# The last stage of a decoder step moved into the experts' phase, with four of nine tiles summed by TensorE products

## The chip, the cores and the metric

The kernel runs on one core of a Trainium2 chip. The metric is the device time of one execution in microseconds (us). The kernel before was timed in three runs; one more execution was profiled.

## The reference, cut to what matters

One step of a hybrid decoder layer over 1024 prompt rows and 64 sample rows, all of width 1024. After the token mixers and the memory attention comes a mixture of experts, and then a last norm:

```
eid, comb = hier_route(hn, ...)          # two experts of 32 for each row, and their two weights
h = h + routed_experts(hn, eid, comb, w_e_gate, w_e_up, w_e_down)
y = rmsnorm(h, g_final)                  # h * rsqrt(mean(h*h) + EPS) * g_final
```

For each row the last stage computes h + c0 * y1 + c1 * y2, where y1 and y2 are the results of the row's two experts, and then scales the row by its root mean square and by g_final. Everything before this stage is the same in both kernels.

## The kernel before, in words

The 1088 rows lie in TILES = 9 tiles of P = 128 rows; the last holds 64 rows. `build` calls phases one after the other; between two stands `core.end_phase()` (L129), which clears the semaphores and lets all engines meet at a barrier. Each phase's block ends with a meeting of the engines too.

`phase_experts` (L2324) runs the 32 experts. Each gets one block of 128 gathered rows; its result `y` is copied by ScalarE (L2626) and stored to `blocks` in HBM by ScalarE's DMA queue (L2628), with a count on `y_stored0` or `y_stored1`. Rows beyond 128 of one expert would go to extra blocks: `over_blocks` (L2355) is a loop of NOVER = 16 rounds on each engine, with a branch around its body in each round, taken where there is no such block. Here there is none, so each engine goes through 16 rounds that do nothing. TensorE goes through them after its last product (L2537), VectorE after L2590, ScalarE after its last store (L2677), GpSimd much earlier (L2446). SyncE loads h into `h_rows` (L2411) and g_final into `g_rows` (L2412) at the end of the phase. ScalarE waits for the last stores at L2679.

`phase_combine` (L2682) is the last stage. GpSimd issues 18 indirect DMAs (L2704), two for each tile, which gather y1 and y2 from `blocks` into SBUF, and only then, behind them in its own queue, the nine small powers (L2710, mean square to the power -0.5). VectorE's order is written out: for tile t `add(t)` (L2719 and L2720, each one operation over 1024 columns), `mean_square(t - 1)` (L2724), `gain(t - 2)` (L2729). ScalarE squares and sums a tile (L2751) and scales it (L2746, `normed`). SyncE stores each tile when `gain` is done (L2697).

Before the change VectorE's part of one tile is:

```
lk(v.scalar_tensor_tensor(h[r, t], y1[r, t], comb[r, 0, t:t + 1], h[r, t], ALU.mult, ALU.add))
v.scalar_tensor_tensor(h[r, t], y2[r, t], comb[r, 1, t:t + 1], h[r, t], ALU.mult, ALU.add)
v.tensor_tensor(o[r, t], o[r, t], gf[r], ALU.mult)
```

Of the kernel before, what the change touches and what calls it, by code (L numbers as in the profile page):

```python
# [13 lines left out]
ALU = mybir.AluOpType  # L14
ACT = mybir.ActivationFunctionType
AX = mybir.AxisListType
F32 = mybir.dt.float32
# [3 lines left out]
P = 128  # L21
D = 1024
KC = D // P
SEQ = 1024
DB, DS = 8, 8
NS = DB * DS
# [2294 lines left out]
                ins.then_inc(S_("table"), 1)  # L2321


def phase_experts(core, PS, slot_tok, over_info, raw, wg_hi, wg_lo, h_rows, g_rows):  # L2324

# [9 lines left out]
    GU, DN = range(0, 4), range(4, 6)  # L2335
    with ExitStack() as ctx:
        sb = lambda n, s, t=F32: ctx.enter_context(nc.sbuf_tensor("ex_" + n, s, t))
        wd_hi, wd_lo = sb("wd_hi", [P, len(DN), PW], F32R), sb("wd_lo", [P, len(DN), PW], F32R)
        w_hi = lambda j: wg_hi[:, j] if j in GU else wd_hi[:, j - len(GU)]
        w_lo = lambda j: wg_lo[:, j] if j in GU else wd_lo[:, j - len(GU)]  # L2340
        xg = sb("xg", [P, 2, D])
        x_hi, x_lo = sb("x_hi", [P, 2, KC, P], F32R), sb("x_lo", [P, 2, KC, P], F32R)
# [44 lines left out]
        with nc.Block() as block:  # L2387
            @block.sync
            def _(sp):
                sp.dma_start(ident[:], d["ident"]).then_inc(S_("ident"), 16)  # L2390
                for j in range(NP):
                    sp.sem_inc(S_(f"w{j}"), 16)

                def load_gu(n, freed):
                    for j in GU:
                        sp.wait_ge(S_("w_split"), freed(j))
                        sp.dma_start(raw[:, j], expert_piece(d, j, n)).then_inc(S_(f"w{j}"), 16)

                def load_dn(n):
                    for j in DN:  # L2400
                        sp.wait_ge(S_("w_split"), done_dn(n - 1, j))
                        sp.dma_start(raw[:, j], expert_piece(d, j, n)).then_inc(S_(f"w{j}"), 16)

                load_gu(1, lambda j: j + 1)
                with sp.Fori(2, NE) as n:
                    load_gu(n, lambda j: done_gu(n - 1, j))
                    load_dn(n - 1)
                load_dn(NE - 1)
                sp.wait_ge(S_("w_used"), done_gu(LAST, GU[-1]))
                for t in range(TILES):  # L2410
# [10 lines left out]
                sp.wait_ge(S_("h_rows"), 16 * (TILES + 1))  # L2421

            @block.gpsimd
            def _(po):
# [15 lines left out]
                def over(j):  # L2440
                    po.wait_ge(S_("ov_turned"), j)
                    po.tensor_copy(idx[:, 0:1], slot_tok[:, bass.ds(j + NE, 1)]).then_inc(S_("ov_idx"), 1)
                    po.wait_ge(S_("ov_idx"), j + 1)
                    po.sem_inc(S_("passed"), 1)
                    po.indirect_dma_start(xg[:, 0], None, d["hn"], bass.IndirectOffsetOnAxis(ap=idx[:, 0:1], axis=0)).then_inc(S_("ov_rows"), 16)
                over_blocks(po, over)  # L2446

            @block.tensor
            def _(pe):
# [85 lines left out]
                    ins.then_inc(S_("ov_d"), 1)  # L2535
                pe.wait_ge(S_("y"), NE + 1)
                over_blocks(pe, over)  # L2537

            @block.vector
            def _(v):  # L2540
# [51 lines left out]
                def over(j):  # L2592
# [5 lines left out]
                    v.wait_ge(S_("ov_d"), j)  # L2598
                    v.tensor_copy(hT[:], h_in()).then_inc(S_("ov_hT"), 1)
                over_blocks(v, over)  # L2600

            @block.scalar
            def _(act):
# [74 lines left out]
                for par in range(2):  # L2678
                    act.wait_ge(S_(f"y_stored{par}"), 16 * (NE // 2) + 16)  # L2679


def phase_combine(core, PS, dest, comb, h, gf):  # L2682

    nc, d, sem = core.nc, core.dram, core.sem
    S_ = lambda n: sem("cb_" + n)
    with ExitStack() as ctx:
        sb = lambda n, s, t=F32: ctx.enter_context(nc.sbuf_tensor("cb_" + n, s, t))
        y1, y2, o = sb("y1", [P, TILES, D]), sb("y2", [P, TILES, D]), sb("o", [P, TILES, D])
        expo, st = sb("expo", [P, 1]), sb("st", [P, TILES, 4])
        rows = [P if t < NT else NS for t in range(TILES)]  # L2690
        with nc.Block() as block:  # L2691
            @block.sync
            def _(sp):
                for t in range(TILES):
                    sp.wait_ge(S_("out"), t + 1)
                    dst = d["y_p"][t * P:(t + 1) * P, :] if t < NT else d["y_s"]
                    sp.dma_start(dst, o[0:rows[t], t]).then_inc(S_("stored"), 16)  # L2697
                sp.wait_ge(S_("stored"), 16 * TILES)

            @block.gpsimd  # L2700
            def _(po):
                for t in range(TILES):
                    for k, y in enumerate((y1, y2)):
                        po.indirect_dma_start(y[0:rows[t], t], None, d["blocks"],  # L2704
                                              bass.IndirectOffsetOnAxis(ap=dest[0:rows[t], k, t:t + 1], axis=0)).then_inc(S_(f"y{t}"), 16)
                po.memset(expo[:], -0.5).then_inc(S_("expo"), 1)  # L2706
                po.wait_ge(S_("expo"), 1)
                for t in range(TILES):
                    po.wait_ge(S_("ms"), t + 1)
                    po.tensor_tensor(st[:, t, 2:3], st[:, t, 1:2], expo[:], ALU.pow).then_inc(S_("rstd"), 1)  # L2710

            @block.vector
            def _(v):
                lk = Steps(v, S_("dve"))

                def add(t):
                    r = slice(0, rows[t])
                    v.wait_ge(S_(f"y{t}"), 32)
                    lk(v.scalar_tensor_tensor(h[r, t], y1[r, t], comb[r, 0, t:t + 1], h[r, t], ALU.mult, ALU.add))  # L2719
                    v.scalar_tensor_tensor(h[r, t], y2[r, t], comb[r, 1, t:t + 1], h[r, t], ALU.mult, ALU.add).then_inc(S_("added"), 1)  # L2720

                def mean_square(t):
                    v.wait_ge(S_("squares"), t + 1)
                    v.tensor_scalar(st[:, t, 1:2], st[:, t, 0:1], 1.0 / D, EPS, ALU.mult, ALU.add).then_inc(S_("ms"), 1)  # L2724

                def gain(t):
                    r = slice(0, rows[t])
                    v.wait_ge(S_("normed"), t + 1)
                    v.tensor_tensor(o[r, t], o[r, t], gf[r], ALU.mult).then_inc(S_("out"), 1)  # L2729

                for t in range(TILES):
                    add(t)
                    if t >= 1:
                        mean_square(t - 1)
                    if t >= 2:
                        gain(t - 2)
                mean_square(TILES - 1)
                gain(TILES - 2)
                gain(TILES - 1)

            @block.scalar
            def _(act):
                def normed(t):
                    r = slice(0, rows[t])
                    act.wait_ge(S_("rstd"), t + 1)
                    act.activation(o[r, t], h[r, t], ACT.Copy, scale=st[r, t, 2:3]).then_inc(S_("normed"), 1)  # L2746

                for t in range(TILES):
                    act.wait_ge(S_("added"), t + 1)

                    act.activation(y1[:, t], h[:, t], ACT.Square, accum_out=st[:, t, 0:1]).then_inc(S_("squares"), 1)  # L2751
                    if t >= 1:
                        normed(t - 1)
                normed(TILES - 1)


def build(nc, dram):
    with ExitStack() as ctx:
# [16 lines left out]
        dest, comb = sb("dest", [P, 2, TILES], I32), sb("comb", [P, 2, TILES], F32)  # L2775
        slot_tok, over_info = sb("slot_tok", [P, NBLK], I32), sb("over_info", [P, NOVER + 1], I32)
        with ExitStack() as weights:
            wg_hi, wg_lo = [weights.enter_context(nc.sbuf_tensor("ex_" + n, [P, 4, PW], F32R)) for n in ("wg_hi", "wg_lo")]
        h_rows, g_rows, rest = sb("h_rows", [P, TILES, D], F32), sb("g_rows", [P, D], F32), sb("rest", [P, 6, D], F32)
        with ExitStack() as experts:  # L2780
            raw = experts.enter_context(nc.sbuf_tensor("moe_raw", [P, len(PIECES), PW], F32))
            phase_route(core, PS, dest, comb, slot_tok, over_info, raw)
            core.end_phase()
            phase_experts(core, PS, slot_tok, over_info, raw, wg_hi, wg_lo, h_rows, g_rows)
            core.end_phase()
        phase_combine(core, PS, dest, comb, h_rows, g_rows)


SCRATCH = {"proj": ((ROWS, NIN), F32), "mu_shift": ((DB, NRW), F32), "pm": ((ROWS + 8, NRW), F32), "mixed": ((ROWS, D), F32), "h2": ((ROWS, D), F32),
# [57 lines left out]
```

## Time and profile before

| | us |
|---|---|
| median of 3 runs | 2061.6 (2060.19 to 2062.38) |
| profiled execution, its own time | 2058.51 |
| its span in the profile | 2056.7 |
| PE busy | 1797.1 (87%) |
| DVE busy | 1195.4 (58%) |
| ACT busy | 824.9 (40%) |
| POOL busy | 339.8 (17%) |

PE is TensorE, PEld its weight loads, DVE is VectorE, ACT ScalarE, POOL GpSimd and SP SyncE; a "q" behind a name is that engine's sequencer, which handles branches, waits and the issue of DMAs. Times inside the span are us from its start; lengths in "min/median/max" are ns. The granted clock (PEclk) is a share of TensorE's full 2.4 GHz: 1.00 is that, 0.50 is 1.2 GHz.

### The profile page before, as it was taken

The page shows a single profiled execution, that of the slowest core. Times are in us where ns is not written, and L with a number is a line of the kernel's source. Part 1 is how long each engine was busy: PE and PEld are TensorE (multiplying, and loading weights), DVE is VectorE, ACT ScalarE, POOL GpSimd, SP SyncE. Part 2 cuts the span into 40 slices and gives each one's busy share as a digit, 9 for nine tenths or more (in the row PEclk, how much of TensorE's full clock was granted, in tenths as well). Part 3 has the DMA queues.
Part 4 walks back from the last instruction along what each step waited for, and adds up shares of the span by engine and source line. Part 5 has one row for each costly group of instructions (what it writes and reads, how often), then busy time and mean ns, then how long its engine had stood idle before and what let it go on. Part 6 is the DMA issues. An engine that isn't in the chain of part 4 may idle for free. (4 is left out here: it accounts for less than half of the span.)

```text
span 2056.7 us, 35509 instructions
## 1 busy us (share of the span) xinstructions
PE 1797.1 (87%) x14826; PEld 1477.8 (72%) x14826; DVE 1195.4 (58%) x1320; ACT 824.9 (40%) x930; POOL 339.8 (17%) x307
## 2 busy tenths in 40 slices
PE   7999997988888976899999998728999999999940
PEld 7998885777777755787888885327888888888830
DVE  4533103677777655424333331168989999999926
ACT  5111212434333314302212120017777777777713
POOL 1322002343333420000000000011111111111004
PEclk9999998999999977999999999859999999999975
DMA  7765253222223128552011126159999999999856
GB/s 286 236 201 178 95 166 88 66 72 72 93 76 96 54 57 292 207 196 101 31 42 53 37 102 254 59 206 348 404 405 400 404 401 401 405 401 405 327 190 244
DMA packets 111973, 419.12 MB, mean 204 GB/s; under 512 B 25892, under 2 KB 44264, under 8 KB 82920
## 3 DMA queue, kind: packets, MB, share of 16 engines
q1 hardware_dynamic: 99592, 373.76, 48.7%
q0 software_dynamic: 7072, 25.69, 3.3%
q10 hardware_dynamic: 5184, 17.82, 2.1%
q8 instruction: 100, 1.64, 0.3%
q14 instruction: 25, 0.20, 0.0%
HBM read 350.10 MB, written 75.53 MB: 207 GB/s over the span
## 5 line engine op out<-in xcount | busy, mean ns | idle before, releaser
L2544 DVE TENSOR_TENSOR ex_wg_lo<-moe_raw,ex_wg_hi 128x2048 fp32r<-128x2048 f32 x128 | 287.4, 2284 | 10.7 <-ACT ex_wg_hi L2609 10.5
L2609 ACT CAST ex_wg_hi<-moe_raw 128x2048 fp32r<-128x2048 f32 x128 | 244.6, 1913 | 80.3 <-PE banks L2454 55.4
L2454 PE MATMUL banks<-ex_wg_hi,ex_x_hi 128*128 128x512 f32 x512 | 207.8, 406 | 11.2 <-issue 6.9
L2454 PE MATMUL banks<-ex_wg_hi,ex_x_lo 128*128 128x512 f32 x512 | 201.9, 394 | 0.0
L2454 PE MATMUL banks<-ex_wg_lo,ex_x_hi 128*128 128x512 f32 x512 | 201.2, 393 | 0.0
L2544 DVE TENSOR_TENSOR ex_wd_lo<-moe_raw,ex_wd_hi 128x2048 fp32r<-128x2048 f32 x64 | 146.3, 2288 | 56.0 <-ACT ex_wd_hi L2609 56.0
L2609 ACT CAST ex_wd_hi<-moe_raw 128x2048 fp32r<-128x2048 f32 x64 | 122.3, 1912 | 52.8 <-PE banks L2454 34.1
L2454 PEld LDWEIGHTS banks<-ex_wg_hi,ex_x_hi 128*128 128x128 f32 x512 | 97.3, 190 | 43.1 <-issue 22.1
L516 PE MATMUL banks<-pj_w_hi,pj_x_hi 128*128 128x448 f32 (+1 forms) x288 | 109.7, 381 | 11.2 <-DVE pj_x_lo L347 11.2
L2454 PEld LDWEIGHTS banks<-ex_wg_hi,ex_x_lo 128*128 128x128 f32 x512 | 97.1, 190 | 21.2
L2454 PEld LDWEIGHTS banks<-ex_wg_lo,ex_x_hi 128*128 128x128 f32 x512 | 97.5, 191 | 18.5
L516 PE MATMUL banks<-pj_w_lo,pj_x_hi 128*128 128x448 f32 (+1 forms) x288 | 109.4, 380 | 0.0
L2454 PE MATMUL banks<-ex_wd_hi,ex_h_hi 128*128 128x512 f32 x256 | 102.4, 400 | 6.0 <-DVE ex_h_lo L2556 6.0
L2454 PE MATMUL banks<-ex_wd_hi,ex_h_lo 128*128 128x512 f32 x256 | 102.3, 400 | 0.0
L2454 PE MATMUL banks<-ex_wd_lo,ex_h_hi 128*128 128x512 f32 x256 | 102.1, 399 | 0.0
L2426 POOL COPY ex_idx<-moe_slot_tok 128x1 int32 (+1 forms) x32 | 25.3, 791 | 461.5 <-PE banks L2364 415.5
L1595 POOL TENSOR_TENSOR at_st<-at_st,at_expo 128x1 f32<-128x1 f32 x18 | 9.7, 542 | 532.8 <-DVE at_st L1631 532.8
L516 PE MATMUL banks<-pj_w_hi,pj_x_lo 128*128 128x448 f32 (+1 forms) x256 | 97.4, 380 | 0.0
L1108 PE MATMUL banks<-mx_TTT,mx_X 64*64 64x64 f32 x1344 | 77.6, 224 | 4.6 <-DVE mx_X L744 1.5
L516 PE MATMUL banks<-pj_odd_lo,pj_x_hi 128*128 128x448 f32 (+1 forms) x216 | 81.6, 378 | 0.0
L516 PE MATMUL banks<-pj_odd_hi,pj_x_hi 128*128 128x448 f32 (+1 forms) x216 | 81.6, 378 | 0.0
L1017 ACT COPY mx_TTT<-banks 128x512 f32<-128x512 f32 (+1 forms) x84 | 45.3, 540 | 89.9 <-PE banks L1108 89.0
(403 smaller groups left out, 4111.6 us busy)
## 6 DMA issues: line engine op xcount, KB each, us to landing
moe_raw<-w_e_gate SPq DMA_DIRECT2D x64, 1024.0 KB, 7.8
moe_raw<-w_e_up SPq DMA_DIRECT2D x64, 1024.0 KB, 7.3
moe_raw<-w_e_down SPq DMA_DIRECT2D x64, 1024.0 KB, 7.7
blocks<-ex_y ACTq DMA_DIRECT2D x32, 512.0 KB, 7.8
mx_pin<-proj SPq DMA_DIRECT2D x8, 1664.0 KB, 6.9
h<-at_h SPq DMA_DIRECT2D x18, 512.0 KB, 2.7
at_slots<-cache_mem_k SPq DMA_DIRECT2D x8, 1024.0 KB, 12.0
at_slots<-cache_mem_v SPq DMA_DIRECT2D x8, 1024.0 KB, 7.4
```

The costliest lines, as they stand in the source:

```text
L516: ins = pe.matmul(PS[:, n % 8, 0:width], xs[:, t, k, :], ws[c % 2][:, k, 0:width], start=k == 0 and a == 0, stop=k == KC - 1 and a == len( ...
L1017: act.copy(TTT[:, g].rearrange("p x m t -> p (x m t)")[:, 0:n], PS[:, 2 + g, 0:n]).then_inc(S_("T_ready"), 1)
L1108: return pe.matmul(out, a, b, start=start, stop=stop, skip_group_check=True)
L1595: po.tensor_tensor(rstd_c(par), ms_c(par), expo[:, 0:1], ALU.pow).then_inc(S_(kind + "_rstd"), 1)
L2426: po.tensor_copy(idx[:, bf:bf + 1], slot_tok[:, bass.ds(n, 1)]).then_inc(S_("idx"), 1)
L2454: ins = pe.matmul(out, a, b, start=first and i == 0, stop=final and i == 2)
L2544: v.tensor_tensor(w_lo(j), raw[:, j], as_f32(w_hi(j)), ALU.subtract).then_inc(S_("w_split"), 1)
L2609: act.copy(w_hi(j), raw[:, j]).then_inc(S_("w_high"), 1)
```

## The change

`phase_combine` is gone, and so is the `end_phase` before it; its work stands at the end of `phase_experts`. GpSimd waits for the stores of `blocks` itself, then issues the same 18 gathers and the nine powers. VectorE makes eight diagonal matrices (a row weight times the identity) while it has nothing else, adds five tiles (0, 1, 3, 5, 8) as before, and finishes all tiles with one operation, `scaled(t)`, that multiplies by the row's factor and by g_final together; it comes BEHIND = 5 tiles after the add. ScalarE only squares. For tiles 2, 4, 6 and 7 TensorE forms the sum in PSUM with six f32 products of 512 columns: identity by h, diagonal by y1, diagonal by y2, for each half of the columns. `h_rows`, `g_rows`, `y1` and `y2` lie where the split weights lay.

```
+            @block.gpsimd                       (behind over_blocks)
+                for par in range(2):
+                    po.wait_ge(S_(f"y_stored{par}"), 16 * (NE // 2) + 16)
+                for t in range(TILES):
+                    for k, y in enumerate((y1, y2)):
+                        po.indirect_dma_start(y[0:rows[t], t], None, d["blocks"],
+                                              bass.IndirectOffsetOnAxis(ap=dest[0:rows[t], k, t:t + 1], axis=0)).then_inc(S_(f"y{t}"), 16)
+                po.memset(expo[:], -0.5).then_inc(S_("expo"), 1)
+                po.wait_ge(S_("expo"), 1)
+                for t in range(TILES):
+                    po.wait_ge(S_("ms"), t + 1)
+                    po.tensor_tensor(st[:, t, 2:3], st[:, t, 1:2], expo[:], ALU.pow).then_inc(S_("rstd"), 1)
...
+            @block.tensor                       (behind over_blocks)
+                pe.wait_ge(S_("h_rows"), 16 * (TILES + 1))
+                pe.wait_ge(S_("dg"), 2 * len(ON_PE))
+                for n, t in enumerate(ON_PE):
+                    pe.wait_ge(S_(f"y{t}"), 32)
+                    for hf in range(2):
+                        cols = slice(hf * 512, hf * 512 + 512)
+                        pe.matmul(pair_of(t)[:, hf, :], ident[:], h_rows[:, t, cols], start=True, stop=False)
+                        pe.matmul(pair_of(t)[:, hf, :], dg[:, n, 0, :], y1[:, t, cols], start=False, stop=False)
+                        ins = pe.matmul(pair_of(t)[:, hf, :], dg[:, n, 1, :], y2[:, t, cols], start=False, stop=True)
+                    ins.then_inc(S_("summed"), 1)
...
+            @block.vector                       (behind over_blocks)
+                def scaled(t):
+                    r = slice(0, rows[t])
+                    v.wait_ge(S_("rstd"), t + 1)
+                    src = pair_of(t).rearrange("p a n -> p (a n)") if t in ON_PE else h_rows[r, t]
+                    v.scalar_tensor_tensor(h_rows[r, t], src, st[r, t, 2:3], g_rows[r], ALU.mult, ALU.mult).then_inc(S_("out"), 1)
+                for n, t in enumerate(ON_PE):
+                    for k in range(2):
+                        v.tensor_scalar(dg[:, n, k, :], ident[:], comb[:, k, t:t + 1], None, ALU.mult).then_inc(S_("dg"), 1)
+                v.wait_ge(S_("h_rows"), 16 * (TILES + 1))
+                for t in range(TILES):
+                    if t not in ON_PE:
+                        add(t)
+                    if t >= 1:
+                        mean_square(t - 1)
+                    if t >= BEHIND:
+                        scaled(t - BEHIND)
+                mean_square(TILES - 1)
+                for t in range(TILES - BEHIND, TILES):
+                    scaled(t)
...
+            @block.scalar                       (behind over_blocks; the waits for y_stored are gone here)
+                for t in range(TILES):
+                    if t in ON_PE:
+                        act.wait_ge(S_("summed"), ON_PE.index(t) + 1)
+                    else:
+                        act.wait_ge(S_("added"), t + 1 - sum(u < t for u in ON_PE))
+                    act.activation(y1[:, t], pair_of(t).rearrange("p a n -> p (a n)") if t in ON_PE else h_rows[:, t], ACT.Square, accum_out=st[:, t, 0:1]).then_inc(S_("squares"), 1)
...
-            phase_experts(core, PS, slot_tok, over_info, raw, wg_hi, wg_lo, h_rows, g_rows)
-            core.end_phase()
-        phase_combine(core, PS, dest, comb, h_rows, g_rows)
+            phase_experts(core, PS, slot_tok, over_info, dest, comb, raw, split, final)
```

`add` and `mean_square` are the functions of before. How the rows of the program move is seen at three places. On GpSimd, at the end of the experts' phase; over_info is the number of extra blocks. Before:

```order
L2358 REGISTER_ALU
L2358 COMPARE_AND_BRANCH
L2387 UNCONDITIONAL_BRANCH
L131 ISA [waits barrier_Pool_Activation_PE_DVE_SP_gather]
L2700 UNCONDITIONAL_BRANCH [waits barrier_Pool_Activation_PE_DVE_SP_gather]
L2704 DMA cb_y1<-blocks,moe_dest 128x1024
L2704 DMA cb_y2<-blocks,moe_dest 128x1024
```

Now (the semaphores in brackets bear names of an earlier phase, whose numbers they took over; they are the two `y_stored`):

```order
L2364 REGISTER_ALU
L2364 COMPARE_AND_BRANCH
L2462 DMA moe_y1<-blocks,moe_dest 128x1024 [waits pj_stored4,pj_stored3]
L2462 DMA moe_y2<-blocks,moe_dest 128x1024
```

The first gather no longer stands behind a barrier of all five engines, only behind the two store counts.

On VectorE, in the middle of the last stage. Before, one round of the steady order:

```order
L2719 SCALAR_TENSOR_TENSOR moe_h_rows<-cb_y,moe_comb,moe_h_rows 128x1024
L2720 SCALAR_TENSOR_TENSOR moe_h_rows<-cb_y,moe_comb,moe_h_rows 128x1024
L2724 TENSOR_SCALAR cb_st<-cb_st 128x1
L2729 TENSOR_TENSOR cb_o<-cb_o,moe_g_rows 128x1024
```

Now, from the add of tile 5 to the end (L2650 is `scaled`; its input `banks` is PSUM):

```order
L2639 SCALAR_TENSOR_TENSOR moe_h_rows<-moe_y,moe_comb,moe_h_rows 128x1024
L2640 SCALAR_TENSOR_TENSOR moe_h_rows<-moe_y,moe_comb,moe_h_rows 128x1024
L2644 TENSOR_SCALAR ex_st<-ex_st 128x1
L2650 SCALAR_TENSOR_TENSOR moe_h_rows<-moe_h_rows,ex_st,moe_g_rows 128x1024
L2644 TENSOR_SCALAR ex_st<-ex_st 128x1
L2650 SCALAR_TENSOR_TENSOR moe_h_rows<-moe_h_rows,ex_st,moe_g_rows 128x1024
L2644 TENSOR_SCALAR ex_st<-ex_st 128x1
L2650 SCALAR_TENSOR_TENSOR moe_h_rows<-banks,ex_st,moe_g_rows 128x1024
L2639 SCALAR_TENSOR_TENSOR moe_h_rows<-moe_y,moe_comb,moe_h_rows 64x1024
L2640 SCALAR_TENSOR_TENSOR moe_h_rows<-moe_y,moe_comb,moe_h_rows 64x1024
L2644 TENSOR_SCALAR ex_st<-ex_st 128x1
L2650 SCALAR_TENSOR_TENSOR moe_h_rows<-moe_h_rows,ex_st,moe_g_rows 128x1024
```

Four tiles have no add on VectorE, and the finishing operation of a tile comes five tiles behind; the mean square of tile 7 stands ahead of `scaled(3)`, and five `scaled` are left for the end.

On TensorE, behind the 16 empty rounds, where nothing stood before:

```order
L2566 MATMUL banks<-moe_h_rows,ex_ident 128x512 [waits pj_projected,mx_ret_rn,pj_squares]
L2567 MATMUL banks<-moe_y1,ex_dg 128x512
L2568 MATMUL banks<-moe_y2,ex_dg 128x512
L2566 MATMUL banks<-moe_h_rows,ex_ident 128x512
L2567 MATMUL banks<-moe_y1,ex_dg 128x512
L2568 MATMUL banks<-moe_y2,ex_dg 128x512
L2566 MATMUL banks<-moe_h_rows,ex_ident 128x512 [waits pj_mixer_rows]
```

These are the six products of tile 2, and the first of tile 4, which waits for that tile's gathers.

## Rows read from the trace of the kernel before

**Rows 1.** The chain of waits at the end of the kernel, pieces in order of time

```profile
2000.59 0.94 POOL cb_y L2704
...
2024.05 0.58 POOL cb_st L2710
...
2025.83 1.23 DVE cb_o L2729
...
2052.16 1.13 DVEq L2691
```

**Rows 2.** The last store of blocks, in time; then its DMA time to landing

```profile
1985.82 0.34 ACTq L2628 DMA_DIRECT2D blocks<-ex_y  x1
...
blocks<-ex_y ACTq DMA_DIRECT2D x1, 512.0 KB, 2.6
```

**Rows 3.** Empty rounds and barrier by line: ns min/median/max, first and last start

```profile
L2358 POOLq MOVE  x17: 29/29/39, 1924.2 to 1930.9; - x17
L2358 DVEq COMPARE_BRANCH  x16: 50/56/66, 1975.2 to 1983.1; - x16
L2358 PEldq COMPARE_BRANCH  x16: 86/220/228, 1987.4 to 1998.8; - x16
...
L132 POOLq EVENT_SEMAPHORE  x2: 17/17/17, 1999.7 to 1999.8; - x2
```

**Rows 4.** The gathers: ns min/median/max, first and last start; us to landing

```profile
L2704 POOL DMA_INDIRECT cb_y<-blocks,moe_dest x18: 899/937/1705, 2000.6 to 2022.9; - x18
...
DMA to landing us min/median/max: 4.2/6.1/6.4
```

**Rows 5.** Operations of the last stage in time, on DVE

```profile
2007.15 1.28 DVE L2719 SCALAR_TENSOR_TENSOR moe_h_rows<-cb_y,moe_comb,moe_h_rows 128x1024 f32<-128x1024 f32 x1 [30.96 <-DMA cb_y<-blocks,moe_dest]
2008.47 1.28 DVE L2720 SCALAR_TENSOR_TENSOR moe_h_rows<-cb_y,moe_comb,moe_h_rows 128x1024 f32<-128x1024 f32 x1
```

**Rows 6.** Groups of the last stage: xcount, busy us, mean ns, idle before

```profile
L2751 ACT ACTIVATE cb_y<-moe_h_rows 128x1024 f32<-128x1024 f32 x9 | 9.5, 1055 | 32.7 <-DVE moe_h_rows L2720 32.7
L2751 ACT ACTIVATION_READ_ACCUMULATOR cb_y<-moe_h_rows 128x1 f32 x9 | 1.7, 186 | 0.0
L2710 POOL TENSOR_TENSOR cb_st<-cb_st,cb_expo x9: 538/1452/1459, 2024.0 to 2049.7; 128x1 f32<-128x1 f32 x9
```

**Rows 7.** Full-precision products of 512 columns elsewhere in the kernel, in time

```profile
428.20 1.98 PE L1108 MATMUL banks<-mx_sg,mx_mset 128*128 128x512 f32 x4
428.74 0.19 PEld L1108 LDWEIGHTS banks<-mx_sg,mx_mset 128*128 128x128 f32 x1 [0.24 <-issue]
429.17 0.19 PEld L1108 LDWEIGHTS banks<-mx_sg,mx_mset 128*128 128x128 f32 x1 [0.24 <-issue]
...
L2088 PE MATMUL banks<-at_slots,at_bT x64: 592/592/1062, 1288.0 to 1309.5; 128*32 128x512 f32 x64
```

**Rows 8.** Stretches: us, PE, PEld, DVE, ACT, POOL busy, granted clock, DMA

```profile
1291.00:1292.00 1.00, 1.00 (x3) 0.18 (x3) 0.00 (x0) 0.00 (x0) 0.00 (x0) 0.50 0.00 0
1293.00:1294.00 1.00, 1.00 (x8) 0.25 (x4) 0.00 (x0) 0.00 (x0) 0.00 (x0) 1.00 0.00 0
...
1981.00:1982.00 1.00, 1.00 (x4) 0.71 (x4) 0.00 (x0) 0.00 (x0) 0.00 (x0) 0.50 0.00 0
2000.00:2001.00 1.00, 0.00 (x0) 0.00 (x0) 0.00 (x0) 0.00 (x0) 0.41 (x1) 0.50 0.00 0
```

**Rows 9.** One VectorE operation with an input in PSUM; reduced-precision products in time

```profile
L838 DVE SCALAR_TENSOR_TENSOR mx_Ss<-mx_Ss,mx_cdec,banks x2: 1281/1281/1281, 721.5 to 727.0; 128x1024 f32<-128x1024 f32 x2
...
1963.40 0.39 PE L2454 MATMUL banks<-ex_wg_hi,ex_x_hi 128*128 128x512 f32 x1
1963.62 0.39 PE L2454 MATMUL banks<-ex_wg_lo,ex_x_hi 128*128 128x512 f32 x1
1976.29 0.77 PE L2454 MATMUL banks<-ex_wd_hi,ex_h_hi 128*128 128x512 f32 x1 [6.01 <-DVE ex_h_lo L2556]
```

More of the change, by code:

```diff
@@ L2321, in _, with phase_experts @@
                 ins.then_inc(S_("table"), 1)
-def phase_experts(core, PS, slot_tok, over_info, raw, wg_hi, wg_lo, h_rows, g_rows):
+def phase_experts(core, PS, slot_tok, over_info, dest, comb, raw, split, final):
     nc, d, sem = core.nc, core.dram, core.sem
@@ L2337, in phase_experts @@
         sb = lambda n, s, t=F32: ctx.enter_context(nc.sbuf_tensor("ex_" + n, s, t))
-        wd_hi, wd_lo = sb("wd_hi", [P, len(DN), PW], F32R), sb("wd_lo", [P, len(DN), PW], F32R)
+        wg_hi, wg_lo, wd_hi, wd_lo, x_hi, x_lo = split
+        h_rows, g_rows, y1, y2 = final
+        expo, st = sb("expo", [P, 1]), sb("st", [P, TILES, 3])
+        rows = [P if t < NT else NS for t in range(TILES)]
+        BEHIND = 5
+        ON_PE = (2, 4, 6, 7)
+        pair_of = lambda t: PS[:, 2 * ON_PE.index(t):2 * ON_PE.index(t) + 2, :]
+        dg = sb("dg", [P, len(ON_PE), 2, P])
         w_hi = lambda j: wg_hi[:, j] if j in GU else wd_hi[:, j - len(GU)]
@@ L2341, in phase_experts @@
         xg = sb("xg", [P, 2, D])
-        x_hi, x_lo = sb("x_hi", [P, 2, KC, P], F32R), sb("x_lo", [P, 2, KC, P], F32R)
         idx = sb("idx", [P, 2], I32)
@@ L2420, in _ @@
                 over_blocks(sp, over)
-                sp.wait_ge(S_("h_rows"), 16 * (TILES + 1))
+                for t in range(TILES):
+                    sp.wait_ge(S_("out"), t + 1)
+                    dst = d["y_p"][t * P:(t + 1) * P, :] if t < NT else d["y_s"]
+                    sp.dma_start(dst, h_rows[0:rows[t], t]).then_inc(S_("stored"), 16)
+                sp.wait_ge(S_("stored"), 16 * TILES)
             @block.gpsimd
@@ L2445, in over @@
                     po.indirect_dma_start(xg[:, 0], None, d["hn"], bass.IndirectOffsetOnAxis(ap=idx[:, 0:1], axis=0)).then_inc(S_("ov_rows"), 16)
+                    po.wait_ge(S_("ov_finished"), j + 1)
                 over_blocks(po, over)
+                for par in range(2):
[9 more added lines that the diff above has]
+                    po.tensor_tensor(st[:, t, 2:3], st[:, t, 1:2], expo[:], ALU.pow).then_inc(S_("rstd"), 1)
             @block.tensor
@@ L2600, in _, with add, mean_square @@
                 over_blocks(v, over)
+                lk = Steps(v, S_("dve"))
+                def add(t):
+                    r = slice(0, rows[t])
+                    v.wait_ge(S_(f"y{t}"), 32)
+                    lk(v.scalar_tensor_tensor(h_rows[r, t], y1[r, t], comb[r, 0, t:t + 1], h_rows[r, t], ALU.mult, ALU.add))
+                    v.scalar_tensor_tensor(h_rows[r, t], y2[r, t], comb[r, 1, t:t + 1], h_rows[r, t], ALU.mult, ALU.add).then_inc(S_("added"), 1)
+                def mean_square(t):
+                    v.wait_ge(S_("squares"), t + 1)
+                    v.tensor_scalar(st[:, t, 1:2], st[:, t, 0:1], 1.0 / D, EPS, ALU.mult, ALU.add).then_inc(S_("ms"), 1)
+                def scaled(t):
+                    r = slice(0, rows[t])
+                    v.wait_ge(S_("rstd"), t + 1)
[15 more added lines that the diff above has]
+                    scaled(t)
             @block.scalar
@@ L2677, in _ @@
                 over_blocks(act, over)
[L2678 to L2693, printed above, removed]
-                for t in range(TILES):
[L2695 to L2754, printed above, removed]
@@ L2777, in build @@
         with ExitStack() as weights:
-            wg_hi, wg_lo = [weights.enter_context(nc.sbuf_tensor("ex_" + n, [P, 4, PW], F32R)) for n in ("wg_hi", "wg_lo")]
-        h_rows, g_rows, rest = sb("h_rows", [P, TILES, D], F32), sb("g_rows", [P, D], F32), sb("rest", [P, 6, D], F32)
+            shapes = {"wg_hi": [P, 4, PW], "wg_lo": [P, 4, PW], "wd_hi": [P, 2, PW], "wd_lo": [P, 2, PW], "x_hi": [P, 2, KC, P], "x_lo": [P, 2, KC, P]}
+            split = [weights.enter_context(nc.sbuf_tensor("ex_" + n, s, F32R)) for n, s in shapes.items()]
+        final = sb("h_rows", [P, TILES, D], F32), sb("g_rows", [P, D], F32), sb("y1", [P, TILES, D], F32), sb("y2", [P, TILES, D], F32)
         with ExitStack() as experts:
```

## The prediction

> **What bounds the kernel now.** I read the chain of waits first, because only its last stretch is touched. It shows the last stage as three pieces in a row: GpSimd issues gathers from 2000.59, VectorE starts its finishing work at 2025.83, and VectorE's last operation begins at 2052.16 [rows 1]. Then I asked what the first gather waits for. The last store of `blocks` is issued at 1985.82 and has landed 2.6 us later, at 1988.4 [rows 2]. TensorE has passed its 16 empty rounds only at 1998.8, since a branch takes its sequencer up to 0.22 us; the barrier lets go at 1999.8 [rows 3]. So from 1988.4 to 2000.59, 12.2 us, all data is there and only TensorE's empty rounds and the meeting of the engines hold the gathers back. GpSimd itself had passed its rounds at 1930.9 [rows 3].
>
> In the stage itself the 18 gathers start between 2000.6 and 2022.9, one each 1.315 us on average, and one takes about 6.1 us to land [rows 4]. VectorE adds tile 0 from 2007.15, with two operations of 1.28 us [rows 5]; after three tiles it must wait for the first power, which GpSimd starts only at 2024.05, behind all gathers [rows 1]. From 2025.83 on VectorE is busy to the end: 27.5 us to 2053.3, while its own order is the bound.
>
> **The profiled execution** took 2058.51 us with a span of 2056.7; it lies 3.1 us below the median 2061.6. I make the sum on the span and take the difference from the median. A measurement of this kernel tells a change from none at about 0.2%, 4.1 us.
>
> **The change, part by part.** Below, T is the time since the first gather.
>
> *The start.* GpSimd waits for the landing at 1988.4. How quickly it goes on after such a wait has no row of its own. Lower bound: nothing; upper bound: 0.79 us, from the barrier's 1999.8 to 2000.59, which has a branch in it that is gone now [rows 1, 3]. I take 0.5, between the two and nearer the row. T = 0 is 1988.9 instead of 2000.6: **11.7 us saved**, if the rest takes as long. Nobody waits at GpSimd behind this wait but the gathers and powers.
>
> *The gathers* are the same 18. The second of tile t starts at T = 1.315 (2t + 1) and has landed 6.1 later: tile 0 at 7.4 (the row of VectorE's start, 2007.15, allows 6.6), 1 at 10.0, 2 at 12.7, 3 at 15.3, 4 at 17.9, 5 at 20.6, 6 at 23.2, 7 at 25.8, 8 at 28.5. The powers can begin at T = 23.5 as before [rows 1]. Three tiles are added inside the stream before (0, 1, 2) and three now (0, 1, 3), so I leave its pace alone.
>
> *The diagonals.* Eight operations on 128 columns. VectorE has passed its empty rounds at 1983.1 [rows 3]; even at 1.28 us each, what 1024 columns cost, they end by 1993.4, ahead of the first landing at 1988.9 + 7.4 = 1996.3. Cost nothing; the cover is VectorE's idle time, 31 us before [rows 5].
>
> *TensorE's products.* A full-precision product of 512 columns shows as two records; at full clock their weight loads follow each other at 0.43 us (428.74, 429.17) [rows 7]. Six products are 12 records: **5.16 us a tile** at the full level. The clock stands at 0.50 when the first tile lands [rows 8]. Elsewhere such work, begun at 1288.0 in the lower level, ran at 0.50 still at 1291 to 1292 and at 1.00 from 1293 [rows 7, 8]; the other case, from 1976.29, was at 0.50 until 1982 [rows 8, 9]. I take 5 us at half speed, which costs 2.5 us once. TensorE's empty rounds, now without anyone waiting, end at 1998.8, and tile 2 lands at 1988.9 + 12.7 = 2001.6, so they cost nothing; if they ran 3 us longer they would begin to count. Sums are ready at T = 12.7 + 5.16 + 2.5 + a little = **20.5 (tile 2), 25.6 (4), 30.8 (6), 35.9 (7)**. Tiles 4, 6 and 7 have landed by then: TensorE is never waiting again, so its own pace sets these times.
>
> *ScalarE* squares a tile in 1.06 + 0.19 us [rows 6], in order of tiles, so tile 3 waits for tile 2. It no longer scales (nine operations saved, off the path).
>
> *VectorE.* One add is 2.6 us [rows 5]. `scaled` is one operation over 1024 columns with a scalar, as in [rows 9], 1.28 us also with one input in PSUM; back to back I count 1.25. In its written order: add 0 to 10.0, add 1 to 12.7, two mean squares, add 3 to 17.9. Then mean square 2 must wait for tile 2's sum and its squares: 21.9. Mean square 3 follows at 23.2, add 5 to 25.8, mean square 4 (sum at 25.6) at 27.1, `scaled(0)` to 28.3, `scaled(1)` to 29.7, mean square 6 (sum at 30.8) at 32.2, `scaled(2)` to 33.5, add 8 to 36.1, mean square 7 (sum at 35.9) at 37.3, `scaled(3)` to 38.6, mean square 8, and five more `scaled`: **T = 45.0**. Before, VectorE ended at 2053.3 - 2000.6 = 52.7. **7.7 us saved.** GpSimd's powers take up to 1.46 us beside VectorE's work [rows 6], which five tiles of distance cover. What was late before (VectorE waiting for the first power) is gone; late next are TensorE's sums, four times.
>
> *The end* is the same: 3.4 us from VectorE's end to the end of the span.
>
> Sum: 1988.9 + 45.0 + 3.4 = 2037.3, against 2056.7: 19.4 us less. From the median: **2042.2 us**. The loop of the 32 experts has the same instructions; other addresses for the split weights are costed at nothing, because no row shows a product or an operation that depends on its address.
>
> **A rule weighed.** The row says 0.86 us for a full-precision product of 512 columns at full clock [rows 7], where the experts' reduced-precision products follow each other at 0.23 us and less (1963.40, 1963.62) [rows 9]. The Trainium skill (VectorE: DVE Perf Modes, the section on the TRN2 errata) gives a matmul max(60, 6+FD) cycles whatever the type, which is 0.22 us for 512 columns. By that rule the sum would be about 6 us shorter; by the row it is the one above. I go by the row.
>
> **The rivals.**
>
> A, *the products are cheap*: 12 records at 0.23 us, or six, so at most 2.8 us a tile, and TensorE waits for landings instead. Then VectorE is the bound: its end comes at T = 38.8, and the time is 2042.2 - 6.2 = 2036.0. For it: the pace of [rows 9]; against it: [rows 7], the same number format. This is also what the skill's cycle rule gives. 0.04.
>
> B, *the gathers still start late*: something that the rows don't show (the loading of code, a wait for both stores) holds GpSimd to about 2000.6, so only the second part is gained: 2042.2 + 11.7 = 2053.9. Against it: both counts are complete at 1988.4. 0.04. A milder one, the stream of gathers a fifth slower, since it now runs beside other timings: 2.5 to 3 us more, 2045; one gather took 1.7 us for 0.94 [rows 4]. It is part of my range.
>
> C, *TensorE stays at the lower level*: each tile 10.3 us, the four sums end at T = 54, VectorE at 63.1: 18.2 us more, 2060.4, no change that can be told. For it: the clock is at 0.50 at the start. Against it: both cases in [rows 7 to 9] rose within 6 us of such work. The Trainium skill (TensorE: Matmul & The Clock Gate, Part 1) has activity release the clock; this trace agrees, with 1.00 from 1293 on [rows 8]. 0.04.
>
> D, *slower*: the lower level and no overlap of records. If each of the 12 takes its longest record, 1.06 us [rows 7], one after the other, a tile costs 12.8 us on TensorE, and VectorE's in-order mean squares of 2, 4, 6 and 7 wait for each. Its end is T = 73.1: 2042.2 + 28.1 = 2070.3. The kernel is level at 10.6 us a tile and slower by 0.2% from 11.7 on. Against it: 592 ns is the usual record and starts lie closer than ends. 0.02.
>
> **How the numbers follow.** The forecast's own range: the start 0.5 either way, the rise of the clock 0.5, the stream of gathers up to 3, and the spread of runs, 2.2 between the three shown: 2039 to 2046.5, chance 0.86. The full range reaches towards A and towards a slower stream or a drift of the loop: 2037 to 2049. It leaves out B, C and D, most of A, and a tail of the forecast. Faster by over 0.2%: forecast, A and B, 0.94; within 0.2%: C, 0.04; slower: D, 0.02.
>
> **What would show each step.** First gather at 1989 of the span, right after the landing; TensorE's last empty round still near 1999. On TensorE 48 records of f32 products, those of tile 2 at 0.50 and then 1.00, at 0.43 us from start to start; the last ends near 2025. VectorE waits for ScalarE's squares, and through them for TensorE, four times, the first near 2007 to 2011. Then five `scaled` in a row to 2034. Wrong would be: a first gather after 1995, records twice as far apart to the end, or VectorE without any wait for squares.

## The result and the profile after

The changed kernel took 2039.13 us (median of 4 runs, 2034.12 to 2044.39) against 2060.89 for the kernel before: ratio 0.9896, 95% interval 0.9868 to 0.9924. The forecast was 2042.2, with a range of 2037 to 2049. Timed again later beside other kernels (label h2_after below) it came to 0.9883 [0.9866, 0.9899].

The profiled execution took 2034.12 us with a span of 2032.2, 24.5 us less than before. The end of its chain of waits, pieces in order of time (start, us, what):

```profile
1981.69 2.62 DMA blocks<-ex_y
...
1984.35 0.75 issue
1985.11 0.94 POOL moe_y L2462
...
1991.32 6.37 DMA moe_y<-blocks,moe_dest
1997.68 0.14 issue
1997.82 2.04 PE banks L2566 x2
...
2019.41 0.87 PE banks L2568 x2
...
2020.31 1.02 ACT moe_y L2748
...
2021.61 1.19 DVE moe_h_rows L2650
...
2025.25 3.57 DVE moe_h_rows L2650 x3
```

It answers to [rows 1]. The chain no longer goes through a barrier and all 18 gathers but through the last store, six gathers, and then without a gap through TensorE's 24 products, the squares of tile 7 and VectorE's last operations. The lines of the empty rounds, of the gathers and of the finishing operation (ns min/median/max, first and last start; us to landing) answer to [rows 3, 4]:

```profile
L2364 PEldq COMPARE_BRANCH  x16: 86/220/233, 1983.3 to 1994.7; - x16
...
L2462 POOL DMA_INDIRECT moe_y<-blocks,moe_dest x18: 897/938/1801, 1985.1 to 2007.7; - x18
...
DMA to landing us min/median/max: 5.7/6.3/6.8
...
L2650 DVE SCALAR_TENSOR_TENSOR moe_h_rows<-moe_h_rows,ex_st,moe_g_rows x5: 1267/1275/1276, 2011.2 to 2027.6; 128x1024 f32<-128x1024 f32 x4, 64x1024 f32<-64x1024 f32 x1
L2650 DVE SCALAR_TENSOR_TENSOR moe_h_rows<-banks,ex_st,moe_g_rows x4: 1274/1275/1277, 2016.4 to 2026.4; 128x1024 f32<-128x1024 f32 x4
```

TensorE still leaves its empty rounds 13 us after the store, but nobody waits for it. VectorE's operations in time, at the four places where it waited longest for ScalarE (the wait is in brackets):

```profile
2006.01 0.15 DVE L2644 TENSOR_SCALAR ex_st<-ex_st 128x1 f32<-128x1 f32 x1 [3.16 <-ACT moe_y L2748]
...
2011.16 0.15 DVE L2644 TENSOR_SCALAR ex_st<-ex_st 128x1 f32<-128x1 f32 x1 [1.45 <-ACT moe_y L2748]
...
2016.31 0.15 DVE L2644 TENSOR_SCALAR ex_st<-ex_st 128x1 f32<-128x1 f32 x1 [2.55 <-ACT moe_y L2748]
...
2021.46 0.15 DVE L2644 TENSOR_SCALAR ex_st<-ex_st 128x1 f32<-128x1 f32 x1 [1.31 <-ACT moe_y L2748]
```

The four are 5.15 us apart, and each is the mean square of a TensorE tile (2, 4, 6, 7). These are the four waits of the forecast. Two shorter ones are left out: 1.15 us for the squares of tile 1, and 0.88 us for those of tile 3, which ScalarE may only take behind tile 2's.

**Three lengths to read.** The time of a whole execution moves by several us because of phases that the change doesn't touch. In 13 profiled executions of this study the last store of `blocks` was issued between 1981.7 and 1989.9 us. So I read each profile by three numbers: from that issue to the first gather, from the first gather to VectorE's end, and from the issue to the end of the span. Each ratio is to runs of the kernel before that were timed together with that kernel; their medians lay between 2059.63 and 2061.12.

| kernel | store at | to first gather | gather to VectorE's end | store to end | median of runs | ratio to before |
|---|---|---|---|---|---|---|
| before | 1985.8 | 14.8 | 52.7 | 70.9 | 2060.89 | |
| the change | 1981.7 | 3.4 | 43.7 | 50.5 | 2039.13 | 0.9896 [0.9868, 0.9924] |
| h2_after (the change again) | 1982.4 | 3.4 | 43.8 | 50.7 | 2035.76 | 0.9883 [0.9866, 0.9899] |
| e1_meet | 1982.0 | 14.0 | 45.2 | 62.7 | 2049.07 | 0.9946 [0.9929, 0.9962] |
| h1_before_no_rounds | 1989.9 | 10.0 | 52.9 | 66.2 | 2056.39 | 0.9978 [0.9968, 0.9987] |
| e2_no_pe | 1983.7 | 3.4 | 43.4 | 50.2 | 2037.31 | 0.9889 [0.9873, 0.9906] |
| e3_old_order | 1986.4 | 3.4 | 52.8 | 59.7 | 2049.14 | 0.9945 [0.9928, 0.9962] |
| f1_no_pe_b2 | 1987.0 | 3.4 | 50.8 | 57.6 | 2045.75 | 0.9923 [0.9907, 0.9940] |
| f2_pe_b2 | 1984.9 | 3.4 | 43.7 | 50.6 | 2037.64 | 0.9886 [0.9870, 0.9903] |
| e4_one_product | 1984.6 | 3.4 | 39.7 | 46.6 | 2033.89 | 0.9872 [0.9855, 0.9888] |
| g1_157 | 1988.5 | 3.4 | 42.2 | 49.0 | 2038.79 | 0.9891 [0.9874, 0.9907] |
| g2_inter | 1984.1 | 3.4 | 40.5 | 47.4 | 2035.87 | 0.9881 [0.9865, 0.9898] |
| h3_267 | 1988.2 | 3.5 | 42.2 | 49.0 | 2038.18 | 0.9883 [0.9864, 0.9902] |

Between the two profiled executions, 20.4 of the 24.5 us lie behind the store (11.4 at the start, 9.0 in the stage). The other 4.1 lie ahead of it, inside that spread; 1.8 of them are in the experts' loop (last section).

### The profile page after: what moved, and what is told of

It is laid out like the page before. It is cut to its first block and busy times, and to the rows that moved or that the text cites. A ratio compares the mean times of both kernels' runs of the same rounds, so it can differ in the third digit from the quotient of the medians.

```text
span 2032.2 us, 35572 instructions
## 1 busy us (share of the span) xinstructions
PE 1813.5 (89%) x14874; PEld 1485.9 (73%) x14874; DVE 1187.4 (58%) x1320; ACT 814.2 (40%) x921; POOL 335.9 (17%) x307
## 5 line engine op out<-in xcount | busy, mean ns | idle before, releaser
L2576 DVE TENSOR_TENSOR ex_wg_lo<-moe_raw,ex_wg_hi 128x2048 fp32r<-128x2048 f32 x128 | 287.3, 2283 | 10.7 <-ACT ex_wg_hi L2674 10.5
L2436 POOL COPY ex_idx<-moe_slot_tok 128x1 int32 (+1 forms) x32 | 23.7, 742 | 461.3 <-PE banks L2370 415.4
```

Of the source, the lines that this page charges most:

```text
L2436: po.tensor_copy(idx[:, bf:bf + 1], slot_tok[:, bass.ds(n, 1)]).then_inc(S_("idx"), 1)
L2576: v.tensor_tensor(w_lo(j), raw[:, j], as_f32(w_hi(j)), ALU.subtract).then_inc(S_("w_split"), 1)
```

## The experiments

### What held the first gather back

Two kernels put one cause back, or take it out. e1_meet adds to the change:

```
                over_blocks(pe, over)
+                pe.sem_inc(S_("rounds_done"), 1)
...
                    po.wait_ge(S_(f"y_stored{par}"), 16 * (NE // 2) + 16)
+                po.wait_ge(S_("rounds_done"), 1)
```

> The changed kernel, but GpSimd's first gather also waits until TensorE has passed its 16 empty rounds; nothing else differs. Read: the time from the issue of the last store of blocks to the first gather (12.2+2.6=14.8 us before, 3.4 after the change) and to the end of the span (70.9 before, 50.5 after). My theory: TensorE's empty rounds held the gathers back before, so the first gather comes 13.8 us after the store and the end 10.4 us later than with the change: 60.9 us, and some 10 us less than the kernel before in the runs. Rival: the start was set by something else (loading of code, the data itself), so the wait costs under 3 us and the end stays near 50 to 53.

h1_before_no_rounds takes one line out of the kernel before:

```
                pe.wait_ge(S_("y"), NE + 1)
-                over_blocks(pe, over)
```

> The kernel before, with one line taken out: TensorE does not go through the 16 rounds for extra blocks (none exists here, so nothing that the other engines wait for is left out; with extra blocks it would be). Barrier and stage stay. Theory: the barrier itself is cheap and TensorE's rounds, 0.72 us each, were what it waited for; now ScalarE's rounds, passed 8.1 us after the store, set it, so the first gather comes 9.6 to 9.9 us after the last store, not 14.8, and the whole is 5 us shorter than before. Rival (meeting, clearing and the new block cost the time themselves): the first gather stays at 13 us or later.

Measured: the first gather comes 14.0 us after the store in e1_meet, against the expected 13.8, and 10.0 in h1_before_no_rounds, against 9.6 to 9.9. In e1_meet this is the chain of waits at that place, and TensorE's branches by line:

```profile
1988.26 0.22 PEldq L2364
1995.22 0.75 issue
1995.97 0.94 POOL moe_y L2463
...
L2364 PEldq COMPARE_BRANCH  x16: 86/218/228, 1983.6 to 1994.9; - x16
```

In h1_before_no_rounds it is now ScalarE that comes last, and the barrier lets go about 1 us behind it:

```profile
L2358 ACTq COMPARE_BRANCH  x16: 40/45/53, 1991.4 to 1997.9; - x16
...
L132 POOLq EVENT_SEMAPHORE  x2: 17/17/17, 1999.0 to 1999.0; - x2
...
1999.85 0.94 POOL L2703 DMA_INDIRECT cb_y<-blocks,moe_dest  x1 [86.69 <-PEq L2690]
```

So the barrier itself was cheap: from ScalarE's last branch to the first gather it is 1.9 us. Both rivals fall: of the 11.4 us that the change gains at the start, 10.6 come back with nothing but the wait for TensorE's rounds. In the runs, taking the line out gains 4.6 us, near the 5 expected: a ratio of 0.9978 [0.9968, 0.9987].

One number of e1_meet was off: 45.2 us from the first gather to VectorE's end, where I had counted 43.7. TensorE's clock goes with it. Tile 2's six products take 5.16 us at the upper level. In the change they ran from 1997.82 to 2004.66, 6.8 us, and in e1_meet from 2008.75 to the start of the next tile's at 2016.99, 8.2 us, so here the lower level (1.2 GHz) cost 3.1 us and not 1.7. Two stretches of e1_meet, on its line of windows (stretch in us; busy us of PE, weight loads, DVE, ACT and POOL with their counts; granted clock; DMA share; GB/s), show the clock still at half in the fourth us of the products, and little above it in the sixth:

```profile
2012.00:2013.00 1.00, 1.00 (x2) 0.34 (x1) 0.96 (x2) 0.00 (x0) 0.71 (x1) 0.50 0.87 291
2014.00:2015.00 1.00, 1.00 (x3) 0.49 (x2) 0.00 (x0) 0.00 (x0) 0.69 (x2) 0.59 1.06 332
```

### The start alone, and the start without the products

e3_old_order is the change with the order of before: `ON_PE = ()`, `BEHIND = 2`, and two operations to finish a tile again, on ScalarE and VectorE:

```
-                    v.scalar_tensor_tensor(h_rows[r, t], src, st[r, t, 2:3], g_rows[r], ALU.mult, ALU.mult)
+                    v.tensor_tensor(y2[r, t], y2[r, t], g_rows[r], ALU.mult)
...
+                    act.activation(y2[r, t], h_rows[r, t], ACT.Copy, scale=st[r, t, 2:3]).then_inc(S_("normed"), 1)
```

> The stage moved as in the change, but with the order of before: all adds on VectorE, ScalarE scales, VectorE multiplies by the gain two tiles behind. Theory: the start alone is worth 11.4 us (gathers 3.4 us after the store, not 14.8), and the rest lasts as before, 52.7 us from the first gather to VectorE's end: end of the span 59.5 us after the store. Rival (part of the early start is given back because the stream of gathers or GpSimd's queue sets the end): 62 us or more.

e2_no_pe only takes TensorE out:

```
-        ON_PE = (2, 4, 6, 7)
+        ON_PE = ()
```

> The changed kernel with no tile on TensorE: VectorE adds all nine, the finishing operation stays five tiles behind. Theory: with the first gather early and the finishing operation single and five tiles behind, VectorE has enough idle time while gathers land; the products replace a wait for the adds by a wait for TensorE. From the first gather to VectorE's end 43.7 us, as with the change (43.7), the same time within 1 us. Rival (the products carry the second part of the gain, as the change's words suggest): four adds of 2.5 us more on VectorE, 50 to 54 us, 6 to 10 us slower than the change.

Measured: e3_old_order 52.8 us (expected 52.7) and 59.7 from store to end (59.5); the start keeps its full value and gives nothing back. e2_no_pe 43.4 us (43.7), 0.3 less than with the products. The rival, 50 to 54, falls: **five tiles behind, the four tiles on TensorE bring nothing**. VectorE's waits in e2_no_pe, longest first, show why (us in total, times, longest):

```profile
DVE moe_h_rows L2638 <- DMA moe_y<-blocks,moe_dest: 19.7, 3, 18.6
...
DVE moe_h_rows L2649 <- issue: 1.5, 1, 1.5
```

and in the change:

```profile
DVE moe_h_rows L2639 <- DMA moe_y<-blocks,moe_dest: 12.2, 3, 10.3
DVE ex_st L2644 <- ACT moe_y L2748: 10.5, 6, 3.2
```

Without products VectorE adds tiles 0 to 5 while the gathers land, and is then busy to the end, with one pause of 1.5 us. With them it is spared four adds of 2.5 us and waits 10.5 us for squares instead, 8.5 of it for TensorE's tiles. (The longest wait in each list is for the rows of tile 0 and begins before the first gather; it is the shorter one in the change because the diagonals are made first.)

### Products and distance: two remedies for one wait

f1_no_pe_b2 changes both lines, f2_pe_b2 the first alone:

```
-        BEHIND = 5
-        ON_PE = (2, 4, 6, 7)
+        BEHIND = 2
+        ON_PE = ()
```

> The changed kernel with no tile on TensorE and the finishing operation two tiles behind, not five. Theory: the in-order wait of VectorE for the first power (behind all gathers in GpSimd's queue, about 24 us after the first gather) is what cost the time before; two tiles behind, VectorE stops after three adds and six adds are left: 51.5 us from the first gather to VectorE's end, nearly the 52.8 of the old order, 8 us more than five tiles behind without TensorE (43.4). Rival (the single finishing operation is what gains): near 44.

> The changed kernel (four tiles on TensorE) with the finishing operation two tiles behind. Theory: products and distance are two remedies for the same wait, so either alone does what both do: 43.9 us from the first gather to VectorE's end against 51.5 without the products at this distance, and against 43.7 of the change. Rival (the products are useless at any distance, as they were five tiles behind): 50 us or more.

Measured: 50.8 us without the products and 43.7 with them, two tiles behind (expected 51.5 and 43.9). Five tiles behind it was 43.4 and 43.7. The wait of 8.9 us that does it, in f1_no_pe_b2, in time:

```profile
2005.33 0.15 DVE L2643 TENSOR_SCALAR ex_st<-ex_st 128x1 f32<-128x1 f32 x1
2014.41 1.29 DVE L2649 SCALAR_TENSOR_TENSOR moe_h_rows<-moe_h_rows,ex_st,moe_g_rows 128x1024 f32<-128x1024 f32 x1 [8.93 <-POOL ex_st L2468]
```

VectorE stops for the first power, which stands behind all gathers on GpSimd, with six adds (tiles 3 to 8) still to come; most of their rows land during that wait. Five tiles of distance fill that wait with adds; the products take adds away, so that fewer are left behind it. Each alone is worth 7.1 to 7.4 us, both together no more. Against e3_old_order (52.8), which is also two tiles behind and without products, the single finishing operation in f1_no_pe_b2 brings 2.0 us. So the 9.0 us of the stage are 2.0 for that operation and 7 for either remedy.

### TensorE's pace

e4_one_product leaves out two of the three products:

```
-                        pe.matmul(pair_of(t)[:, hf, :], ident[:], h_rows[:, t, cols], start=True, stop=False)
-                        pe.matmul(pair_of(t)[:, hf, :], dg[:, n, 0, :], y1[:, t, cols], start=False, stop=False)
```

> The changed kernel with one of the three products in each half of tiles 2, 4, 6 and 7: identity by h and diagonal by y1 are left out, so a tile costs TensorE 1.7 us and not 5.2. Theory: TensorE's pace set VectorE's four waits, so VectorE's end comes at 38.7 us (39.9 if the clock never rises) after the first gather, not 43.7: 5 us less. Rival (the landings or VectorE's own work set the end): within 1 us of 43.7.

Measured: 39.7 us, 4.0 less than the change, between the two figures expected and near the one for a clock that never rises. TensorE's products in time:

```profile
2000.67 3.43 PE L2566 MATMUL banks<-moe_y,ex_dg 128*128 128x512 f32 x4 [17.14 <-DMA moe_y<-blocks,moe_dest]
2005.70 1.98 PE L2566 MATMUL banks<-moe_y,ex_dg 128*128 128x512 f32 x4 [1.60 <-DMA moe_y<-blocks,moe_dest]
2011.63 6.66 PE L2566 MATMUL banks<-moe_y,ex_dg 128*128 128x512 f32 x8 [3.95 <-DMA moe_y<-blocks,moe_dest]
```

TensorE now waits for landings. The last wait, 3.95 us, has a price: the granted clock, 1.00 from 2004 to 2010, is 0.50 again from 2011 to 2017, and the eight records of tiles 6 and 7 take 6.66 us, where eight at 0.43 would take some 3.4. So in the change the bound was its pace of full-precision products, 5.15 us a tile, while the rows of a tile land every 2.6 us.

### Versions made to beat the change

g1_157 has one tile fewer on TensorE:

```
-        ON_PE = (2, 4, 6, 7)
+        ON_PE = (1, 5, 7)
```

> The changed kernel with three tiles on TensorE, 1, 5 and 7, not four (2, 4, 6, 7). Theory: TensorE's pace (5.16 us a tile, and the lower clock at the start) set four waits, and fewer, spread tiles let it keep up with the landings: 41.2 to 42.5 us from the first gather to VectorE's end, 1 to 2.5 us less than the change's 43.7. Rival (each tile taken from VectorE is worth 2.5 us, so one less costs): 45 to 46.

g2_inter has `ON_PE = (3, 6, 7)`, `BEHIND = 2`, and on GpSimd:

```
-                for t in range(TILES):
-                    po.wait_ge(S_("ms"), t + 1)
-                    po.tensor_tensor(st[:, t, 2:3], st[:, t, 1:2], expo[:], ALU.pow).then_inc(S_("rstd"), 1)
+                powers = {6: (0, 1), 7: (2,), 8: (3, 4, 5, 6, 7, 8)}
...
+                    for u in powers.get(t, ()):
+                        po.wait_ge(S_("ms"), u + 1)
+                        po.tensor_tensor(st[:, u, 2:3], st[:, u, 1:2], expo[:], ALU.pow).then_inc(S_("rstd"), 1)
```

> A version made to beat the change: tiles 3, 6 and 7 on TensorE, the finishing operation two tiles behind, and GpSimd takes the first powers between gathers (0 and 1 behind the gathers of tile 6, 2 behind tile 7's). Theory: behind TensorE's pace the next bound is the powers' place behind all gathers, so VectorE can finish tiles from 20 us on and ends 38.7 to 39.7 us after the first gather, 4 to 5 us less than the change. Rival (the powers between gathers delay the stream, and GpSimd waits for VectorE in turn): 43 to 44, nothing gained.

h3_267 has other tiles and distances, and the mean squares two tiles behind:

```
-        BEHIND = 5
-        ON_PE = (2, 4, 6, 7)
+        BEHIND = 3
+        ON_PE = (2, 6, 7)
...
+                powers = {6: (0,), 7: (1,), 8: (2, 3, 4, 5, 6, 7, 8)}
...
-                    if t >= 1:
-                        mean_square(t - 1)
+                    if 2 <= t < TILES + 2:
+                        mean_square(t - 2)
```

> A second version made to beat the change: tiles 2, 6 and 7 on TensorE, the finishing operation three tiles behind, mean squares two tiles behind, powers 0 and 1 between the gathers (behind those of tiles 6 and 7). Theory: with VectorE's waits for squares moved back it is 39.2 to 40.5 us from the first gather to VectorE's end, against 40.5 of the first such version and 43.7 of the change; the total 3 to 4 us below the change. Rival (the stream of gathers plus one tile's chain is already the bound near 40.5): no better than 40.5.

Measured: g1_157 42.2 us, 1.5 less than the change with a tile fewer on TensorE, inside what was expected. g2_inter 40.5, which is 3.2 less than the change but 0.8 more than the upper figure expected. h3_267 42.2, a miss: expected 39.2 to 40.5. GpSimd in g2_inter, in time:

```profile
2006.14 1.11 POOL L2469 TENSOR_TENSOR ex_st<-ex_st,ex_expo 128x1 f32<-128x1 f32 x2
2007.43 1.49 POOL L2465 DMA_INDIRECT moe_y<-blocks,moe_dest  x1 [0.18 <-issue]
...
2010.19 0.75 POOL L2469 TENSOR_TENSOR ex_st<-ex_st,ex_expo 128x1 f32<-128x1 f32 x1
2011.13 1.51 POOL L2465 DMA_INDIRECT moe_y<-blocks,moe_dest  x1 [0.19 <-issue]
```

The gathers right behind a power take 1.5 us and not 0.94, and the last gather is issued 25.4 us after the first (22.5 in the change), so part of what VectorE gains is given back by later landings. The powers alone take 1.9 us of GpSimd's time there. Whether a power makes the gather behind it longer isn't shown: both long ones also run beside VectorE's operations, and in the change one of 1.5 us has no power ahead of it. The rows of tile 7 landed 30.1 us after the first gather, against 26.9 in the change, so TensorE waited 0.9 us for them, and VectorE 1.5 us for the squares of tile 7.

In h3_267 the last gather is issued 26.1 us after the first, but that is not what made it miss. VectorE waits once more at the end, and TensorE's products show why:

```profile
2015.40 2.07 PE L2567 MATMUL banks<-moe_h_rows,ex_ident 128*128 128x512 f32 x2 [3.96 <-DMA moe_y<-blocks,moe_dest]
2017.27 1.91 PE L2568 MATMUL banks<-moe_y,ex_dg 128*128 128x512 f32 x2
...
2023.53 1.02 PE L2567 MATMUL banks<-moe_h_rows,ex_ident 128*128 128x512 f32 x2
...
2030.02 0.15 DVE L2645 TENSOR_SCALAR ex_st<-ex_st 128x1 f32<-128x1 f32 x1 [2.46 <-ACT moe_y L2746]
```

The wait is for the mean square of tile 7, whose products stand directly behind tile 6's. Tile 6's begin at 2015.40, after TensorE has stood idle for 3.96 us; its granted clock, 1.00 from 2008 to 2014, is 0.50 from 2015 to 2021. So tile 6 takes 8.1 us and not 5.15, and tile 7 starts at 2023.53, though its rows had landed at 2019.6. Tile 6's rows were not late either: they landed 23.7 us after the first gather, as in the change (23.9). Without the 3.0 us of the lower clock the wait of 2.46 would be gone, and VectorE's end would come near 39.7, inside what was expected; that is an estimate from these rows, no run shows it. The expectation did not count a lower clock in the middle of the stage. In g1_157 it came back too, 1 to 2 us after tile 5's products had begun behind a pause of 2.8 us (0.50 from 2015 to 2017), and that tile took 6.95 us. In the change TensorE never stops between its four tiles, and the clock stays at 1.00.

In the median times g2_inter, h3_267, e2_no_pe and the change overlap: ratios from 0.9881 to 0.9896, with intervals of 0.0016 and more to each side. The 3 us of g2_inter are shown by the stage of one profile, not by the runs; that it beats the change as a whole isn't shown. It does beat the kernel before, as all of these do.

h2_after is the change without an edit, timed once more beside h3_267.

> The change once more, beside the next kernel and the kernel before on the same chip, to see how far its time moves by what is ahead of the stage. From the last store of blocks to the end 50.5 us within 1.5 us (the rise of TensorE's clock moves it); what is ahead of the store varies by up to 5 us between executions, with the kernel before as well.

That run gave 50.7 us from store to end, and a median 3.4 us below that of the first four runs of the same kernel. That median, 2035.76, lies below the range of the forecast.

## Why the prediction was right, and where its sizes were off

*The start* (11.7 us forecast): 11.4 measured. The landing took 2.6 us as before; GpSimd went on 0.75 us after it, near the upper bound of 0.79, where I had taken 0.5. The reason given, TensorE's empty rounds, is shown by e1_meet and h1_before_no_rounds.

*The gathers*: the last was issued 22.5 us after the first, against 22.4 before; a landing took 6.3 us against 6.1. The term held.

*The diagonals*: eight operations in 1.7 us, from 1979.80, ahead of the store and hidden.

*TensorE's products*: full-precision products are two records each at 0.43 us, a tile 5.15 us (5.16 forecast). Tile 2's six products took 6.8 us, from 1997.82 to 2004.66, so the lower clock cost 1.7 us where I had 2.5; in e1_meet, by the tile's start at 2008.75 and the next at 2016.99, it cost 3.1. The last sum was squared from 35.2 us after the first gather on (35.9). Rivals A and C are out: the products are not cheap, and the clock rises. The cycle table of the Trainium skill (VectorE: DVE Perf Modes, the section on the TRN2 errata) gives one formula for a product and names no number format; an estimate from it is 0.22 us for 512 columns. The stage shows 0.86 us at a granted clock of 1.00, so for full-precision products the measurement decides.

*VectorE*: `scaled` takes 1.28 us from PSUM as from SBUF and goes on every 1.19 us, where I counted 1.25. Its end came at 43.7, against 45.0: 0.7 us of the difference come from the earlier sums, the rest from the pace of the last operations.

*The end*: 3.4 us, as forecast. Sum from store to end: 50.5 measured, 51.5 forecast (3.1 + 45.0 + 3.4). Rivals B (a late start) and D (slower) did not happen. The places in the span that the forecast names (the first gather at 1989, the last product near 2025, VectorE's end at 2034) all came 4 to 5 us earlier, most of it because the store itself came 4.1 us earlier.

*The median*, 2039.13, is 3.1 us below the forecast of 2042.2, and the second one, 2035.76, is 6.4 below and outside the range of 2037 to 2049. So that the first four runs fell into the range is in part luck. The stage itself, from store to end, accounts for 1.0 us. The rest is of the size by which the time ahead of the store moves, and two terms of the sum were too small there. The spread of runs was taken as 2.2 us, from three runs; the four of the change lie 10.3 us apart, and the store moves by 8 us (1981.7 to 1989.9 over 13 executions). And the experts' loop was costed at nothing, but was 1.7 us shorter in the mean in the profiles with the new placement.

What the prediction did not say is which part of the change earns the second 9 us. It counted the adds that TensorE takes over and the waits that it brings in one sum, which was right, but no term asked what the same order would do without TensorE. The runs give the answer: 2.0 us come from the single finishing operation, and 7 from the distance of five tiles or from the products, whichever is there; the second of the two adds nothing.

## What to carry to other kernels

When two parts of a change cure the same wait, try each alone: here moving work off VectorE and giving it other work to do during the wait were each worth 7 us, and together no more. Before a barrier is blamed, look at which sequencer comes to it last and what it was doing; loops of empty rounds have a price on each engine, and here it was highest on TensorE. When work is given to TensorE in pieces, count the lower clock again for a piece that follows a pause: in h3_267 it cost 3.0 us in the middle of the stage. And when a kernel's untouched phases move by more than the difference in question, read the stage from an event just ahead of it.

## What the runs showed of the hardware

- A round of an empty loop (two branches, a move and a register operation) took TensorE's sequencer 0.76 us, ScalarE's 0.44: (1998.8 - 1987.4) / 15 and (1993.9 - 1987.3) / 15, since 16 branches have 15 gaps, with a branch at 220 ns in the median against 45. I had not looked for such a difference. (The expectation of h1_before_no_rounds has 0.72, from a division by 16.)
- The price of TensorE's lower clock at a start is not fixed, and the length of the pause ahead does not order it. The first tile's six products, 5.15 us at the upper level, took 7.9 us after 14.7 us with nothing on TensorE (g1_157), 6.8 after 17.2 (the change), 7.1 after 19.8 (g2_inter) and 8.2 after 27.9 (e1_meet). What does order it stays open.
- The lower clock can come back within the stage. Before tiles that followed pauses of 0.9 to 1.6 us (g2_inter, e4_one_product) the granted clock stayed at 1.00; after pauses of 2.8 us (g1_157), 3.95 (e4_one_product) and 3.96 (h3_267) it was 0.50 for part of the next tile or all of it.
- GpSimd's gathers, 0.94 us in the median, took up to 1.8 us in the change and 2.0 in h3_267. In all 13 profiles each gather longer than 1.1 us ran beside an operation of VectorE over 1024 columns, but most gathers that did stayed below 1.1, so what makes the difference is open. It happened to few of the 18, and the stream hardly changed until powers were put between them.
- The experts' loop, from its first to its last transposing product of gathered rows, took 561.8 and 561.6 us in the two profiles with the old placement of the split weights, and 559.1 to 560.8 in the eleven with the new one. It is 1.7 us in the mean, of the same instructions. No run here tells whether the addresses do it, so the cause stays open.
